# A mixture-of-experts decoder step: ordering the features of the activation in TensorE's reads

## The reference

```
def expert_block(args):
    e, tok = args
    xb = x_pad[tok]
    hgu = xb @ moe_w_gu[e] + moe_b_gu[e]            # 1024 -> 2048
    gate, up = hgu[:, :D_EXPERT], hgu[:, D_EXPERT:]
    gate = jnp.minimum(gate, SWIGLU_LIMIT)
    up = jnp.clip(up, -SWIGLU_LIMIT, SWIGLU_LIMIT)
    act = (up + 1.0) * gate * jax.nn.sigmoid(SWIGLU_ALPHA * gate)
    return act @ moe_w_down[e] + moe_b_down[e]      # 1024 -> 1024
```

## Time and profile before

| | |
|---|---|
| median of 3 runs | 1222.32 us (1220.51 to 1222.92) |
| the profiled execution | 1220.0 us |
| its span, first to last instruction | 1218.3 us |
| mean granted clock of TensorE | 0.989 |
| TensorE busy | 1154.0 us, 95% of the span |
| VectorE busy | 392.2 us, 32% |
| ScalarE busy | 279.0 us, 23% |
| chain that ended last | PE 58%, DMA 31%, DVE 6% |
| moved by DMA | 456.98 MB, mean 375 GB/s |

### The profile page before, as it was taken

The page is one execution under the profiler, slowest core; times in us unless marked ns, Lnnn a source line. Parts: engine busy times, 40 slices in busy tenths (PEclk is TensorE's granted clock), DMA queues, the critical chain, the costliest instruction groups (busy, mean ns, idle before and its releaser), DMA issues.

```text
span 1218.3 us, 16550 instructions
## 1 busy us (share of the span) xinstructions
PE 1154.0 (95%) x6720; PEld 627.1 (51%) x6720; DVE 392.2 (32%) x718; ACT 279.0 (23%) x506; POOL 23.2 (2%) x47
## 2 busy tenths in 40 slices
PE   9999999999999999999999998999999999998996
PEld 8999789994434343434344443434343434343432
DVE  5888587763221212122213110221212121212114
ACT  5686354433202010101010110111010101010101
POOL 1000011001000000000000000000000000000000
PEclk9999999999999999998999998999999999999999
DMA  9736478977999999999999999999999999999995
GB/s 282 247 111 201 142 238 271 349 286 286 424 428 427 427 429 426 428 427 429 424 428 428 429 426 426 427 427 428 428 428 429 427 428 427 429 427 427 429 428 196
DMA packets 76830, 456.98 MB, mean 375 GB/s; under 512 B 5920, under 2 KB 44944, under 8 KB 49296
## 3 DMA queue, kind: packets, MB, share of 16 engines
q1 hardware_dynamic: 73888, 447.04, 89.9%
q0 software_dynamic: 2832, 9.28, 2.4%
q10 hardware_dynamic: 64, 0.03, 0.0%
HBM read 450.38 MB, written 5.95 MB: 375 GB/s over the span
## 4 chain that ended last, share of the span: by engine, by line
PE 58%; DMA 31%; DVE 6%; issue 3%; ACT 1%; SPq 0%; DVEq 0%; ACTq 0%
DMA gu_w<-in_moe_w_gu 31%; PE pool L1031 22%; PE pool L950 9%; PE pool L654 5%; PE pool L655 5%; PE pool L656 5%; PE ub L884 2%; DVE Sg L1867 1%; PE pool L970 1%; PE ob L981 1%; PE pool L931 1%; DVE arena L1864 1%; ACT wh L1163 1%; PE pool L1142 1%; PE ob L1044 1%
## 5 line engine op out<-in xcount | busy, mean ns | idle before, releaser
L1031 PE MATMUL pool<-gu_w,arena 128*64 128x512 f32 x1920 | 428.7, 599 | 27.1 <-DMA gu_w<-in_moe_w_gu 24.3
L1031 PEld LDWEIGHTS pool<-gu_w,arena 128*64 128x64 f32 x1920 | 138.4, 138 | 306.0 <-issue 252.1
L1857 DVE TENSOR_SCALAR arena<-pool 128x512 f32<-128x512 f32 x31 | 21.5, 692 | 623.3 <-PE pool L1031 618.4
L654 PE MATMUL pool<-xh,wh 128*128 128x264 f32 x568 | 163.8, 288 | 1.6 <-DVE arena L1451 0.6
L656 PE MATMUL pool<-xh,wl 128*128 128x264 f32 x568 | 160.7, 283 | 0.0
L1353 ACT ACTIVATE arena<-arena 128x512 f32<-128x512 f32 x32 | 20.2, 630 | 485.6 <-DVE arena L1857 485.6
L950 PE MATMUL pool<-dn_w,arena 128*64 128x512 f32 x512 | 113.6, 595 | 0.9 <-DVE arena L1857 0.9
L654 PEld LDWEIGHTS pool<-xh,wh 128*128 128x128 f32 x568 | 106.9, 188 | 8.5 <-issue 4.4
L655 PE MATMUL pool<-xl_most,wh 128*128 128x264 f32 x385 | 109.2, 284 | 0.0
L656 PEld LDWEIGHTS pool<-xh,wl 128*128 128x128 f32 x568 | 106.5, 187 | 0.0
L950 PE MATMUL pool<-arena 128*64 128x512 f32 x480 | 106.3, 595 | 0.0
(11 more groups left out here) (338 smaller groups left out, 857.9 us busy)
## 6 DMA issues: line engine op xcount, KB each, us to landing
gu_w<-in_moe_w_gu SPq DMA_DIRECT2D x124, 2048.0 KB, 21.5
dn_w<-in_moe_w_down SPq DMA_DIRECT2D x30, 2048.0 KB, 29.9
arena<-in_moe_w_down SPq DMA_DIRECT2D x32, 1024.0 KB, 29.4
arena<-in_moe_w_down SPq DMA_DIRECT2D x15, 2048.0 KB, 27.8
dn_w<-in_w_in SPq DMA_DIRECT2D x24, 1024.0 KB, 6.0
dn_w<-in_w_branch SPq DMA_DIRECT2D x8, 1024.0 KB, 6.0
gu_w<-in_moe_w_gu SPq DMA_DIRECT2D x8, 1024.0 KB, 8.4
gu_w<-in_state_gla POOLq DMA_DIRECT2D x8, 512.0 KB, 6.6
```

The costliest lines, as they stand in the source:

```text
L654: mm(bank(name)[:, 0:T], h[:, k, :], high, start=(k == 0), stop=False)
L1031: last = mm(out, xg[:, k, j * CAP:(j + 1) * CAP], gu_w[:, k, cols], start=False, stop=(k == NB - 1))
L1857: ts(gbuf, gate, LIMIT, None, ALU.min).then_inc(gclip, 1)
```

## The change

The products that fill GATE and UP read their moving operand in another order of columns: for each quarter of 512 columns first the columns 0, 4, 8 and so on, then 1, 5, 9 and so on. A column of PSUM then already holds the feature that the transposes want in its place, and all that VectorE and ScalarE do in between is elementwise. `activate` multiplies without reordering. The number of instructions, their sizes, their waits and all DMAs stay.

```
+            def in_fours(columns):
+
+                return columns.rearrange("p (q a) -> p a q", a=4)
...
                 for out, cols in quarters(GATE, UP):
-                    mm(out, oh[:, :], b3[:, cols], start=True, stop=False)
+                    mm(out, oh[:, :], in_fours(b3[:, cols]), start=True, stop=False)
...
-                        last = mm(out, xg[:, k, 0:CAP], gu_w[:, k, cols], start=False, stop=(k == NB - 1))
+                        last = mm(out, xg[:, k, 0:CAP], in_fours(gu_w[:, k, cols]), start=False, stop=(k == NB - 1))
...
-                            mm(out, oh[:, :], b3[:, cols], start=False, stop=False)
+                            mm(out, oh[:, :], in_fours(b3[:, cols]), start=False, stop=False)
...
-                        last = mm(out, xg[:, k, CAP:2 * CAP], gu_w[:, k, cols], start=(k == 0), stop=(k == NB - 1))
+                        last = mm(out, xg[:, k, CAP:2 * CAP], in_fours(gu_w[:, k, cols]), start=(k == 0), stop=(k == NB - 1))
...
-                        last = mm(out, xg[:, k, j * CAP:(j + 1) * CAP], gu_w[:, k, cols],
+                        last = mm(out, xg[:, k, j * CAP:(j + 1) * CAP], in_fours(gu_w[:, k, cols]),
                                   start=False, stop=(k == NB - 1))
...
-                tt(act_s.rearrange("s (a p) -> s a p", a=4), tbuf.rearrange("s (p a) -> s a p", a=4),
-                   sbuf_.rearrange("s (p a) -> s a p", a=4), ALU.mult).then_inc(act_ready, 1)
+                tt(act_s, tbuf, sbuf_, ALU.mult).then_inc(act_ready, 1)
```

## The result

The changed kernel takes 1666.79 us (median of 4 runs) against 1222.62 for the kernel before: ratio 1.363, 95% interval 1.361 to 1.365. One of its four runs was a slow one of 2983.54 us that the ratio leaves out; the median of the other three is 1665.56. The forecast was 1222 with a range of 1217 to 1640. It was wrong, and the time also lies outside the range. The profiled execution took 1665.6 us, its span is 1663.8.

A forecast was written before the change was run, and what follows sets the result against it. The prediction took the DMA engines' full queue of weight loads as the bound. Profiled 1220.0 us and about 0 for the change made 1220; the runs' median stands 2.3 above, so the forecast was 1222 us, range 1217 to 1640.

The forecast's parts named there:

- What bounds the kernel before: In the experts, 339 to 1160 us, DMA engines are full at 427 to 428 GB/s; freed engine time becomes waits for weights.
- What VectorE saves: VectorE's last product per expert falls from 1087 to 682 ns, 13.0 us in all; TensorE waits 6 us less for it.
- What a step costs TensorE: First products' stepped operand: 0.85 ns a column against 0.83 now, 2.6% or 11 us, hidden by waits for weights.
- the threshold: Time for a pair of first-product passes, put at 458 ns, beyond which the DMA engines are no longer the bound.
- rival 1: First products pay per step as VectorE does, 1.61 to 1.81 ns a column: 1602 or 1706 us; chance 0.23.
- the room: Slack of TensorE before DMA stops being the bound: 24.3 us waits for weights plus 6 us freed, 30 us.
- The upper end of the range: 1640 us, set to reach the rival in which TensorE pays per step as VectorE does, nearly all near 1600.
- The biases: Bias products, 124 passes in 19.9 us; doubled they would add 20 us and still fit by themselves.
- rival 3: Stepped reads disturb DMA writes of loads: 1% off 428 GB/s over 860 us is 9 us, 1231 us; chance 0.05.

The follow-up runs named there:

- no order: Kernel before with VectorE's last product reading and writing contiguous memory and nothing putting the features in order: ratio 0.9999.
- one sixteenth of the products in fours: Kernel before, VectorE contiguous and features unordered, only the gate half of the first of eight weight blocks read in steps of four columns: ratio 1.0025.
- one eighth: Kernel before, VectorE contiguous and features unordered, the first of eight weight blocks of each expert read in steps of four columns: ratio 1.0118.
- the probes: Kernel before with groups of extra products behind its last product, results unused; contiguous float32 over the whole array took 434 ns a pass.
- with twos: Changed kernel with weights and biases in steps of two columns in place of four, VectorE contiguous, features not in the reference's order: ratio 1.0017.
- first probes: Kernel before plus unused products of several types, steps and streams behind its last product; float32 passes took 434 ns contiguous, 450 in twos, 899 in fours.
- second probes: Kernel before plus other unused products, kept at full clock by float32 products ahead, and single copies; rounded float32 took 450 ns in twos, 461 in fours.

## Why the prediction was wrong

- **What bounds the kernel before: right.** The full queue hid all of VectorE's saving (no order: 0.9999) and, but for 0.0025, one sixteenth of the products in fours; one eighth came through.
- **What VectorE saves: right.** Forecast 13.0 us and 6 us less waiting of TensorE; measured 12.6, and 5.5 in the run with no order. In the changed kernel the remaining wait was 0.0, not 4 us, since the longer bias passes cover it.
- **What a step costs TensorE: the step that failed.** The rows gave two readings, 0.85 ns for a column (VectorE's ratio, over TensorE's own full rate) and 1.61 to 1.81 (VectorE's time), and I took the ratio "since the full rates of the engines differ by two". Measured: 1.76 ns. There are two faults in the term. First, 0.48 ns is not the full rate of the operand that changes. The products of the earlier trace rows (L654) read rounded float32 (`xh` and `wh` are F32R in the kernel), one pass each; a pass of true float32 over the whole array takes 434 ns for 512 contiguous columns in the probes, 0.85 ns each, so the experts' passes at 0.83 ran as fast as contiguous float32 runs in any probe, and not at a bit over half the rate. The same ratio over 0.83 gives 1.48 ns, a pair of 757 ns, far above the threshold. Second, the ratio itself is no law: 0.83 to 1.76 is 2.1 and not 1.78, and steps of two cost next to nothing (450 ns for a pair). For float32 and bfloat16 a time for 16 bytes gives all the measured numbers; for rounded float32 in fours it doesn't (0.90 ns). The rows held two hints of a time, 1.61 and 1.81 ns for an element in two operations of VectorE. That these lie so near TensorE's 1.76 is not explained: VectorE with one operand in fours took at most 1.26 ns.
- **The rule of the Trainium skill** (Advanced Engine Details and Errata, SBUF Cachelines), that a line has 16 bytes and needs two hits for the full rate, agrees with the float32 runs: in twos 450 ns against 434, in fours 899. It does not agree with bfloat16 in fours, which has two columns on each 16 bytes and yet takes 449 ns against 218. The rule spoke against the change, and rival 1 got a chance of only 0.23 because the page has no size for it.
- **Rival 1 was the case, its price was off.** It stood at 1602 for 1.61 ns and at 1706 for 1.81. At the measured 900 ns a pair it gives 1220 + 1024 x 0.474 - 30 = 1675, and with 13 us for the biases 1688, 22 above the 1665.6. Part of that is the room, which was more than 30 us (see the run with one eighth). By the two pages: the first products added 472.6 us (457.0 to 929.6), not 485; the biases 13.4; TensorE's idle time fell by 36.6 (64.3 to 27.7), not 30; the rest 4 less. 1220.0 + 472.6 + 13.4 - 36.6 - 4 = 1665.4.
- **A slip in the threshold:** 30 us over 1024 pairs are 29 ns, so it lies at 455 ns for a pair and not at 458. At 900 it changes nothing.
- **The upper end of the range** left out the upper price of rival 1, which rested on the very instruction that the change replaces; a range that reaches to a rival should reach to its dearer price.
- **The biases: half right.** In steps of 8 bytes they cost 0.47 us for an expert as long as nothing covers it, 8 to 9 us in all beyond the room.
- **The loads (rival 3): nil**, as the Trainium skill has it (SBUF — State Buffer, Who interferes with whom): with twos the rate is 426 to 428 GB/s, with one eighth in fours 416 from 339 to 813 us, where TensorE no longer waits for weights, and 428 from 813 to 1160. That it falls to 287 to 294 in the changed kernel is TensorE's late release of buffers: its loads land in 7.7 us, the quickest in 7.5, and the quickest of the kernel before, beside contiguous reads, took 7.6. The busy share fell less than the rate (0.75 of 1.01 against 287 of 427); why is not shown.

## What to carry to other kernels

Price a stepped read by the bytes from one column to the next, and as a time: here 16 bytes cost 1.76 ns on each stream of TensorE, for float32 and bfloat16. A contiguous float32 pass needs 0.85 ns for a column anyway, so a step of 8 bytes (0.88) is nearly free and one of 16 costs the double. Take an engine's full rate from rows of the very type that changes. An order of elements that must be made somewhere belongs where the fewest elements pass: 128 weight loads of the transposes did for nothing what 2048 passes over the weights did for 444 us. A full queue of loads hides a slower engine only up to its waits: here 44 us, of which the profile's idle time showed 33.

## What was not expected of the hardware

- A contiguous stream beside a stepped one is held back with it: a pair took 907 ns with one in fours, 899 with both.
- Rounded float32 pays 0.84 to 0.90 ns for a column in steps of 2, 4 and 8 alike; float32 and bfloat16 pay 1.75 to 1.80 for 16 bytes and more.
- The stepped read did not slow down with the clock. In the first probes the granted clock fell to 0.50, the lower of its two levels (1.2 GHz), while bfloat16 products of 256 columns in steps of 16 bytes ran; their weight loads went on at 0.45 us from one to the next, as before the fall. Contiguous rounded float32 at that clock (L1221) took 427 ns a product against 231 at the full one:

```profile
1320.87 0.12 PEld L1214 LDWEIGHTS pool<-arena,ones 96*128 96x128 bf16 x1 [0.34 <-issue]
1321.33 0.12 PEld L1214 LDWEIGHTS pool<-arena,ones 96*128 96x128 bf16 x1 [0.33 <-issue]
1321.78 0.13 PEld L1214 LDWEIGHTS pool<-arena,ones 96*128 96x128 bf16 x1 [0.33 <-issue]
```

The table for the microsecond from 1321 us on (stretch, busy PE, PEld, DVE, ACT, POOL, PEclk, DMA share, GB/s):

```profile
1321.00:1322.00 1.00, 1.00 (x4) 0.25 (x2) 0.00 (x0) 0.00 (x0) 0.00 (x0) 0.50 0.00 0
```

- The granted clock fell to a mean of 0.57 in the 4 us behind six bfloat16 products in steps of 16 bytes, though TensorE had not been idle (same columns; second probes):

```profile
1264.00:1268.00 4.00, 4.00 (x6) 0.66 (x5) 0.00 (x0) 0.00 (x0) 0.00 (x0) 1.00 0.00 0
1268.00:1272.00 4.00, 4.00 (x7) 1.65 (x6) 0.00 (x0) 0.00 (x0) 0.00 (x0) 0.57 0.00 0
```

  The contiguous float32 passes there (L1215) took 7.03 us for 12, against 5.33 for the same 12 earlier, so they do follow the clock. In the first probes it fell while the bfloat16 eights ran, behind the fours in bfloat16. The changed kernel, whose float32 passes also take one column in 1.76 ns, kept a mean of 0.992, so a slow read alone does not bring it about; what does is not shown.
